# Who issues the partner-row transfers of q and k: from ScalarE's queue to GpSimd's, behind its low parts

## The reference, cut to what matters

```python
proj = xn @ w_in[i]
q, k, v, u, gates = jnp.split(proj, splits, axis=-1)
...
q = rope(rmsnorm(q, q_norm_gain[i]), cos, sin)
k = rope(rmsnorm(k, k_norm_gain[i]), cos, sin)

def rope(t, cos, sin):
    t1, t2 = jnp.split(tf, 2, axis=-1)
    out = jnp.concatenate([t1 * cos - t2 * sin, t2 * cos + t1 * sin], axis=-1)
```

## Time and profile before

| | us |
|---|---|
| median of 3 runs (lowest, highest) | 2069.97 (2069.93, 2071.17) |
| the profiled execution's own time | 2067.69 |
| its span | 2065.9 |
| PE busy / DVE busy / ACT busy / POOL busy | 2027.7 / 1323.9 / 942.2 / 945.9 |
| mean granted clock of TensorE | 0.995 |

### The profile page before, as it was taken

The page is one execution under the profiler, slowest core; times in us unless marked ns, Lnnn a source line. Parts: engine busy times, 40 slices in busy tenths (PEclk is TensorE's granted clock), DMA queues, the critical chain, the costliest instruction groups (busy, mean ns, idle before and its releaser), DMA issues.

```text
span 2065.9 us, 27849 instructions
## 1 busy us (share of the span) xinstructions
PE 2027.7 (98%) x10072; PEld 1629.6 (79%) x10072; DVE 1323.9 (64%) x1979; ACT 942.2 (46%) x1385; POOL 945.9 (46%) x368
## 2 busy tenths in 40 slices
PE   8999999999999999999999998999999999999999
PEld 7875788888888775888888887878776888888887
DVE  5866257787757654268877749975688625464555
ACT  6345464443453446544344353355576444333332
POOL 5433246544645323756566656234322354443442
PEclk9999999999999999999999999999999999999999
DMA  5432213332224331123233333332211323233222
GB/s 189 155 113 74 69 62 102 104 120 99 91 85 155 123 90 62 62 85 118 90 103 111 104 116 103 92 106 94 77 47 62 116 88 101 83 101 102 90 94 82
DMA packets 111858, 202.29 MB, mean 98 GB/s; under 512 B 6544, under 2 KB 51856, under 8 KB 111504
## 3 DMA queue, kind: packets, MB, share of 16 engines
q1 hardware_dynamic: 104800, 189.12, 28.0%
q10 hardware_dynamic: 6960, 11.88, 2.0%
HBM read 189.44 MB, written 8.12 MB: 96 GB/s over the span
## 4 chain that ended last, share of the span: by engine, by line
PE 80%; DVE 10%; issue 4%; ACT 3%; POOL 2%; ACTq 0%; DMA 0%; DVEq 0%; SPq 0%; POOLq 0%
PE bank L796 46%; PE bank L1043 13%; PE bank L1023 7%; PE bank L910 6%; PE bank L1054 2%; PE bank L921 2%; DVE att L2826 1%; POOL w_lo L602 1%; PE bank L868 1%; PE bank L939 1%; DVE att L2809 1%; PE bank L979 1%; DVE w L2686 1%; PE bank L967 1%; PE bank L850 1%
## 5 line engine op out<-in xcount | busy, mean ns | idle before, releaser
L602 POOL TENSOR_TENSOR w_lo<-raw,w_hi 128x2048 fp32r<-128x2048 f32 (+1 forms) x123 | 542.6, 4411 | 827.0 <-ACT w_hi L1544 812.4
L796 PE MATMUL bank<-act_hi,w_hi 128*128 128x512 f32 x1072 | 427.6, 399 | 1.6 <-DVE hid L2894 1.3
L796 PE MATMUL bank<-act_hi,w_lo 128*128 128x512 f32 x1072 | 418.2, 390 | 0.0
L796 PE MATMUL bank<-act_lo,w_hi 128*128 128x512 f32 x1072 | 417.9, 390 | 0.0
L1544 ACT ACTIVATE w_hi<-raw 128x2048 fp32r<-128x2048 f32 (+1 forms) x112 | 203.3, 1815 | 281.0 <-PE bank L796 195.9
L796 PEld LDWEIGHTS bank<-act_hi,w_hi 128*128 128x128 f32 x1072 | 201.5, 188 | 54.6 <-issue 12.4
L796 PEld LDWEIGHTS bank<-act_hi,w_lo 128*128 128x128 f32 x1072 | 201.3, 188 | 43.3
L796 PEld LDWEIGHTS bank<-act_lo,w_hi 128*128 128x128 f32 x1072 | 201.6, 188 | 40.6 <-issue 1.0
L570 POOL TENSOR_TENSOR w_lo<-w_sum,w_hi 128x1024 fp32r<-128x1024 f32 x56 | 133.6, 2406 | 206.0 <-ACT w_hi L1853 192.5
L2563 DVE TENSOR_TENSOR f<-f,bank 128x512 f32<-128x512 f32 x196 | 133.4, 686 | 111.1 <-PE bank L1043 111.1
L1043 PE MATMUL bank<-w_hi,q_hi 128*128 128x512 f32 x392 | 152.7, 390 | 0.5 <-DVE w_lo L2570 0.4
(11 more groups left out here) (427 smaller groups left out, 4131.4 us busy)
## 6 DMA issues: line engine op xcount, KB each, us to landing
raw<-in_w_up SPq DMA_DIRECT2D x32, 1024.0 KB, 5.6
raw<-in_w_down SPq DMA_DIRECT2D x32, 1024.0 KB, 4.9
raw<-in_w_in SPq DMA_DIRECT2D x26, 1024.0 KB, 5.2
raw<-in_w_up SPq DMA_DIRECT2D x44, 512.0 KB, 4.5
raw<-in_w_in SPq DMA_DIRECT2D x28, 768.0 KB, 4.6
raw<-in_w_out SPq DMA_DIRECT2D x12, 1024.0 KB, 5.0
raw<-in_w_down SPq DMA_DIRECT2D x22, 512.0 KB, 4.1
raw<-in_w_attn_proj SPq DMA_DIRECT2D x4, 1024.0 KB, 4.9
```

The lines of the kernel that those rows point to most:

```text
L602: pool.tensor_tensor(m.w_lo[slot][:, 0:n], m.raw[slot][:, 0:n], m.w_hi[slot][:, 0:n].bitcast(F32), ALU.subtract).then_inc(s["split_ready"], 1)
L796: mm = pe.matmul(o, ll if i == 2 else lh, rl if i == 1 else rh, start=first and n == 0, stop=last and n == len(steps) - 1)
```

## The change

`fetch_partner` moves from ScalarE's order to GpSimd's. ScalarE now only counts each block that it has taken out (`q_made`), and GpSimd waits for that count, keeps the wait on `q_ready`, and issues the same four DMAs. In GpSimd's order they come at the same steps p as before in ScalarE's, behind the low part of the step if there is one; `turns(2)` comes behind the transfers of step 7 and `turns(3)` behind those of step 11. The low parts are the same in number (ten are now in the new loop).

```diff
@@ in low_parts (GpSimd)
+    def fetch_partner(j):
+
+        pool.wait_ge(s["q_made"], j + 1)
+        if j >= 2:
+            pool.wait_ge(s["q_ready"], j - 1)
+        block = (m.q2 if j < KD else m.k2)[:, j % KD, :]
+        half = HD // 2
+        for r in range(0, P, half):
+            of = r + half if r % HD == 0 else r - half
+            pool.dma_start(m.partner[j % 2][r:r + half, :], block[of:of + half, :]).then_inc(s[f"partner{j % 2}"], 16)
+
     whole(turns(1))
-    lo()
-    whole(turns(2))
-    lo()
-    whole(turns(3))
-    for _ in range(4):
-        lo()
-    lo()
-    left = U_SECOND - 3 * N_UP2 + 1 - 3 - 8
+    for p in range(4, 44):
+        if p % 4 == 0:
+            lo()
+        for j in jobs_at(p, PARTNER_AT):
+            fetch_partner(j)
+        if p in (7, 11):
+            whole(turns(2 if p == 7 else 3))
+    left = U_SECOND - 3 * N_UP2 + 1 - 3 - 8 - 3
@@ in functions (ScalarE)
         act.activation(block_of(j), bank[b][:], ACT.Copy, scale=gain).then_inc(s[f"free{b}"], 1)
         freed(b)
-
-    def fetch_partner(j):
-
-        if j >= 2:
-            act.wait_ge(s["q_ready"], j - 1)
-        half = HD // 2
-        for r in range(0, P, half):
-            of = r + half if r % HD == 0 else r - half
-            act.dma_start(m.partner[j % 2][r:r + half, :], block_of(j)[of:of + half, :]).then_inc(s[f"partner{j % 2}"], 16)
+        act.sem_inc(s["q_made"], 1)
@@ in jobs(p) (ScalarE)
-        for j in jobs_at(p, PARTNER_AT):
-            fetch_partner(j)
```

More of the change, by code:

```diff
@@ L284 @@
     "q_squared", "q_columns", "q_normed", "q_ready", "partner0", "partner1",
-    "lam_exp", "lam_ready",
+    "q_made", "lam_exp", "lam_ready",
     "o_squared", "o_normed",
```

## The result

The changed kernel takes 2076.88 us (median of 11 runs, 2072.69 to 2079.06), the kernel before 2069.93 in the same batch (11 runs, 2066.07 to 2071.96): ratio 1.0034, 95% interval 1.0026 to 1.0042. It is slower by 7.0 us. The profiled execution took 2073.73 us, its span 2071.8, 6.0 and 5.9 more than before.

A forecast was written before the change was run, and what follows sets the result against it. VectorE's hand-written order, losing time to GpSimd by mutual exclusion, was taken as the bound from 1260 to 1349. Its lateness of 3.8 + 1.7 = 5.5 us gave 2073.2 us profiled, 2075.5 as median; range 2069 to 2092.

The forecast's parts named there:

- my own signs: Right: tables 3 after 1282, rotation 2 later than 1296, TensorE's wait at 1281 shortened; wrong: low part 12 before 1292.
- The price t: GpSimd's time per DMA issue, taken as 1.06 us, bounded by 0.51 and 2.1; a job of four then costs 4.2 us.
- Steps 1 and 3: TensorE waits 2.4 us at piece 12 for low part 8, then 3.8 at piece 16 for low part 12.
- Step 2: VectorE's rotation 1 ends at 1278.7 instead of 1280.48; TensorE's 6.0 us wait shrinks to 2.0, and 1.6 of clock returns.
- Step 4: VectorE in strips 0 and 1: rotation 2 ends 3.8 us late, and a later low part 16 adds 1.7.
- Value on the path: nothing: Taking 64 issues of 0.61 us, 39 us, off ScalarE gains nothing, since no TensorE wait in the stage is for ScalarE.
- The sum: VectorE's lateness of 3.8 + 1.7 = 5.5 us reaches TensorE whole at the stage's last wait: 2073.2 profiled, 2075.5 median.
- Faster: Rival: tables 3 leave VectorE's way, only step 2's gain acts; needs t up to 0.1; about 2065, chance 0.07.
- No change: Rival: issues up to 0.7 us, or low parts 16 and 20 falling on PSUM reads; about 2072, chance 0.33.
- Jobs that don't fit: Rival: t near 2, so GpSimd's jobs and low parts overrun their intervals; 2085 to 2093, chance 0.15.
- Issues that also shut VectorE out: Rival: issues exclude VectorE's SBUF instructions as GpSimd's arithmetic does; 2092, chance 0.06.
- My last sign: Sign of a wrong prediction: low parts late in the blocks of k too, where jobs 11 to 15 have slack.

The follow-up runs named there:

- stand: Changed kernel with a small GpSimd write after each of the 64 issues, so a job of four takes about 4.5 us instead of 2.0: 2073.30 us, ratio 1.0019.
- blank pair: Low parts 12, 16, 20, 24 written as zeros without reading, in the changed kernel and in the kernel before: 2063.66 and 2063.29 us.
- gated_after: Changed kernel with low parts 12, 16, 20, 24 each waiting until VectorE finished stage 2 of strips 0 to 3: 2070.68 us, ratio 1.0002.
- after: The changed kernel itself, transfers issued by GpSimd, against the kernel before: 2076.88 us, ratio 1.0034.

## Why the prediction was right, and where its working failed

The time was right (2076.88 in the range, 1.4 above the forecast, slower as forecast), and half of the working was not. That the number came so close is luck. Of my own signs, low part 12 before 1292 was to mean wrong, and it began at 1283.59; tables 3 began at 1275.38 and rotation 2 ended at 1290.24, where "right" asked for 1282 and 1296; only the shortened wait and VectorE's late last stage 2 came.

**The price t.** 0.50 us against my 1.06. My lower bound, the shortest ScalarE issue, was the right row; GpSimd's shortest arithmetic said nothing about an issue. The Trainium skill's 1 us ("DMA: Bandwidth & Descriptors") tells, in its table of latencies, of the way to the first byte, and my estimate from it took that for the time in the queue; the trace has 0.50 us in the queue and 2.3 us to landing.

**Steps 1 and 3.** Neither wait occurred: low part 8 began at 1259.88 and low part 12 at 1283.59, and TensorE waited 0.4 us for low parts in the whole stage. In stand, with a job as long as mine, waits for low parts did come.

**Step 2** held in direction: rotation 1 ends earlier (4.9 us, I said 1.8) and the long wait shrank to 3.4 (I said 2.0). Its clause that the clock would not fall failed: L1192 ran at 0.50 behind the wait of 3.35 and took 4.64, more than the 3.96 of before.

**Step 4** named the right victim, stage 2 under low part 16, for the wrong reason. I had low part 16 late behind tables 3 and low part 12. It came early, because its high part no longer waited in ScalarE's queue, and I had written of ScalarE's release "Value on the path: nothing". That is the sentence that failed. I then took 1.7 us where 4.7 came, and 1.2 became 4.2 for low part 20, which I had not followed at all.

**The sum** had VectorE 5.5 us late; it ends stage 2 of strip 3 7.4 us later in the stage (128.7 against 121.2), and the profiled executions differ by 6.0. At the measured t my own text gave "2072", 5 us too little, so errors of opposite sign met: t twice too large, and exclusion and clock (4.2 of the 6.2 us is longer busy time) too small.

**The rivals.** "Faster" needed t up to 0.1 and fell as written; yet its mechanism, shown apart in the blank pair, halves TensorE's wait (6.8 to 3.4 us), though the medians there are level. "No change" had the right t but counted on a lucky fall of low parts 16 and 20, and they fell badly. "Jobs that don't fit" is out. "Issues that also shut VectorE out" is out as well: from 1273.41 to 1275.37 four issues run beside stage 2 of strip 0, and L2693 takes 0.68. The rule that two SBUF inputs exclude only GpSimd work that reads SBUF (the Trainium skill, "SBUF — State Buffer", on who interferes with whom) agrees with these rows, and with the blank runs, whose memsets read nothing. My last sign, low parts late in the blocks of k, did not appear.

What stays open: how much of the 4.2 us of longer busy time goes back to the 2.0 us of added waits was not tried apart, and gated_after's remaining loss in stretch 2 was shown to hang on the gate, not which of the late transfer and the excluded rotation weighs more.

## What to carry to other kernels

When transfers leave an engine's queue, ask first what that queue now does earlier, and whom this meets: here a freed ScalarE let GpSimd's 4.6 us subtraction start earlier, onto VectorE's densest place, and the next ones met a late VectorE. Where two engines exclude each other, one count that both know (here `state_ready`) that starts the long instruction under PSUM reads is worth more than moving issues: 0.22% of the kernel before, and none of it without the gate of low part 24. But each gate must be priced for everything queued behind it, as the one at low part 24 showed with transfers behind it and without.

## What was not expected of the hardware

- A DMA of 64 KB from SBUF to SBUF holds GpSimd 0.50 us (64 issues, 0.496 to 0.658), less than it holds ScalarE (median 0.61).
- Waits of 1.97 and 2.01 us in after were each followed by about 3 us at 0.51 to 0.55 of the clock; the one of 1.57 us before L1199 was not (1.52 us for its matmuls, against 2.76 at the earlier trace rows). But the length of a wait alone doesn't say it: in gated_after TensorE stood 3.20 us to 1297.05, and the clock stayed at 1.00. Its windows there, the wait and what follows it:

```profile
1294.00:1297.00 3.00, 0.00 (x0) 0.00 (x0) 2.79 (x5) 0.38 (x1) 0.44 (x1) 1.00 0.28 77
1297.00:1300.00 3.00, 2.95 (x68) 2.73 (x69) 2.97 (x5) 0.00 (x0) 1.55 (x4) 1.00 0.37 87
```

  Behind the first `sums_out`'s wait of 3.4 us, which both kernels have, the clock stayed low for 5.6 us in after and for 3.1 in gated_after. What decides it is open.
- By the start times of the rows, the exclusion takes hold of an instruction that began before the subtraction too: L2695 began at 1297.82, the low part at 1298.03, and it took 5.34 us instead of 0.68.
